# Group norm by ScalarE inside a recurrence, and a gate applied to turned tiles

## The chip, the cores and the metric

One core of a Trainium2 chip runs the whole program: a stack of transformer layers over 512 tokens of width 1,024. The metric is the device time of one execution in microseconds; the kernel before is given by the median of three runs, and its profile is one further execution.

## The reference, cut to what matters

The change lies in the first mixer, RWKV-7, of 16 heads with 64 features each. After the recurrence has made `y`, each head of each token is normed, scaled, given a bonus and a gate, and projected:

```
_, y = lax.scan(_rwkv7_step, S0, ...)              # S = S*w + (S a) b^T + v k^T ; y = S r
ym = y.mean(-1); yv = square(y - ym).mean(-1)      # over the 64 features of a head
yn = (y - ym) * rsqrt(yv + GN_EPS) * lnx_g + lnx_b
bonus = sum(r * k * r_k, -1) * v
g = sigmoid(xg @ g1) @ g2
x = layernorm(ALPHA * x + (1 + gt1) * ((yn + bonus) * g) @ w_out)
```

`gt1` and the shift and scale of the next layer come from a modulation vector `silu(c) @ ada_w + ada_b`, of which four parts of 1,024 columns are summed during the recurrence.

## The kernel before, in words

Three blocks follow one another for this mixer, with a barrier of all engines between them. `rwkv_project` makes receptance, key, value, decay and gate. `rwkv_chunks` runs the recurrence in four turns `t` of 128 tokens. `rwkv_finish` does what comes behind it. Then the feed-forward layer `ffn0` starts. Each engine has its own instruction stream, written out by hand, with semaphores between them; nothing is reordered.

In a turn of `rwkv_chunks` TensorE transposes three operands, forms products with 64x64 matmuls, inverts a triangular matrix in five levels (`LEVELS`), and then forms `UT`, the new state and the output. VectorE masks and adds between these products. ScalarE only copies: three transposed operands (L1365), the output of the turn before (`take_output`, L1370, into `Y`), two halves of `LT` (L1380), `ZA` (L1382, during the first level) and, after the last level, four pieces of `UT` (L1386), which TensorE needs for its next products. Between the `ZA` copy and the `UT` copies it has no work. `take_output(3)` stands behind the last turn and ends the block.

In `rwkv_finish` TensorE first sums the modulation over partitions (eight products with `ones`, L1531). VectorE takes the four tiles `t` of 128 tokens one after the other through a norm of twelve instructions (L1595 to L1614), six in `moments` and six behind them, with ScalarE's square root between. GpSimd multiplies `V` by the bonus factors `BON` (L1521). For each gated tile TensorE does eight transposes (L1541), ScalarE copies them out (L1570, `oT`), and TensorE does 16 products of 512 columns with `w_out` (L1549). `deepnorm_rows` (L531 to L541) then norms the rows on VectorE, beginning after all four tiles are gated. Every operand of L1549 is plain float32, and the profile has two matmul rows for each such product.

## Time and profile before

| | us |
|---|---|
| median of three runs | 2758.96 |
| lowest and highest of them | 2757.99, 2761.84 |
| the profiled execution's own time | 2755.7 |
| its span, first to last instruction | 2753.9 |
| the recurrence, `rwkv_chunks` | about 264 to 504.5 |
| `rwkv_finish` | about 504.7 to 593 |

The page of the profile gives the busy share of the span as 92% for TensorE, 75% for VectorE, 36% for ScalarE and 14% for GpSimd. Those are means over stages with different limits. Times below are counted from the span's start. A row of the timeline has the start, the time and what was idle before with its releaser; consecutive alike instructions stand in one row with their number, so a row of 32 matmuls is 16 products.

### The profile page before, as it was taken

The page shows a single profiled execution, that of the slowest core. Times are in us where ns is not written, and L with a number is a line of the kernel's source. Part 1 is how long each engine was busy: PE and PEld are TensorE (multiplying, and loading weights), DVE is VectorE, ACT ScalarE, POOL GpSimd, SP SyncE. Part 2 cuts the span into 40 slices and gives each one's busy share as a digit, 9 for nine tenths or more (in the row PEclk, how much of TensorE's full clock was granted, in tenths as well). Part 3 has the DMA queues.
Part 4 walks back from the last instruction along what each step waited for, and adds up shares of the span by engine and source line. Part 5 has one row for each costly group of instructions (what it writes and reads, how often), then busy time and mean ns, then how long its engine had stood idle before and what let it go on. Part 6 is the DMA issues. An engine that isn't in the chain of part 4 may idle for free. (4 is left out here: it accounts for less than half of the span.)

```text
span 2753.9 us, 42542 instructions
## 1 busy us (share of the span) xinstructions
PE 2546.2 (92%) x17194; PEld 2000.7 (73%) x17194; DVE 2055.5 (75%) x2896; ACT 989.2 (36%) x1075; POOL 390.5 (14%) x211
## 2 busy tenths in 40 slices
PE   5999988889999989999999988998998999999993
PEld 3785888558888854467788877886578788888883
DVE  6873666788777638778777766985846899999994
ACT  2632111122220023442222004333222777777772
POOL 1000000100000020000000000000002366656651
PEclk8999999999999999999999998999998999999997
DMA  5221122327663281204665323321407899999973
GB/s 209 81 82 41 65 80 80 139 79 227 183 187 126 84 257 53 77 31 136 215 184 174 116 79 112 92 77 47 153 1 260 316 369 372 371 368 360 367 299 129
DMA packets 247801, 459.91 MB, mean 167 GB/s; under 512 B 31125, under 2 KB 205869, under 8 KB 232297
## 3 DMA queue, kind: packets, MB, share of 16 engines
q1 hardware_dynamic: 227592, 433.41, 45.2%
q0 software_dynamic: 14384, 24.25, 2.6%
q8 instruction: 108, 1.77, 0.3%
q10 hardware_dynamic: 5682, 0.20, 0.1%
q14 instruction: 35, 0.29, 0.0%
HBM read 457.28 MB, written 30.56 MB: 177 GB/s over the span
## 5 line engine op out<-in xcount | busy, mean ns | idle before, releaser
L49 PE MATMUL ffn_bank<-ffn_xT_high,ffn_wi_high 128*128 128x512 f32 x704 | 275.4, 391 | 4.2 <-DVE stay_z_r L43 2.7
L50 PE MATMUL ffn_bank<-ffn_xT_low,ffn_wi_high 128*128 128x512 f32 x704 | 275.2, 391 | 0.0
L3304 POOL DMA_INDIRECT expert_rows<-exp_ys,exp_to_row x32 | 155.5, 4861 | 45.3 <-issue 44.4
L49 PEld LDWEIGHTS ffn_bank<-ffn_xT_high,ffn_wi_high 128*128 128x128 f32 x704 | 132.5, 188 | 32.2 <-DVE stay_z_r L43 3.3
L50 PEld LDWEIGHTS ffn_bank<-ffn_xT_low,ffn_wi_high 128*128 128x128 f32 x704 | 132.3, 188 | 28.3
L43 DVE TENSOR_TENSOR moe_u_low<-moe_u,exp_u_high 128x4096 fp32r<-128x4096 f32 x32 | 141.6, 4426 | 13.2 <-ACT exp_u_high L3378 12.8
L43 DVE TENSOR_TENSOR moe_g_low<-moe_g,moe_g_high 128x4096 fp32r<-128x4096 f32 x32 | 141.6, 4425 | 8.8 <-ACT moe_g_high L3378 8.6
L43 DVE TENSOR_TENSOR moe_d_low<-moe_d,exp_d_high 128x4096 fp32r<-128x4096 f32 x32 | 141.4, 4419 | 0.0
L51 PE MATMUL ffn_bank<-ffn_xT_high,stay_z_r 128*128 128x512 f32 x352 | 139.8, 397 | 0.0
L51 PE MATMUL ffn_bank<-ffn_wo_high,ffn_act_low 128*128 128x512 f32 x352 | 138.0, 392 | 0.0
L49 PE MATMUL ffn_bank<-ffn_wo_high,ffn_act_high 128*128 128x512 f32 x352 | 137.7, 391 | 0.0
L51 PE MATMUL ffn_bank<-ffn_xT_high,ffn_wi_low 128*128 128x512 f32 x352 | 137.2, 390 | 0.0
L3378 ACT CAST moe_g_high<-moe_g 128x4096 fp32r<-128x4096 f32 x31 | 112.8, 3639 | 64.4 <-PE exp_p_g L51 64.4
L3378 ACT CAST exp_u_high<-moe_u 128x4096 fp32r<-128x4096 f32 x32 | 116.4, 3637 | 3.8 <-PEq L2997 3.8
L3378 ACT CAST exp_d_high<-moe_d 128x4096 fp32r<-128x4096 f32 x32 | 116.6, 3643 | 1.1 <-DMA moe_d<-in_w_e_down 1.1
L3288 POOL COPY exp_from_row<-exp_rows 128x2 int32 (+1 forms) x30 | 107.9, 3596 | 10.5 <-PE exp_p_x L3332 6.5
L49 PE MATMUL exp_p_g<-moe_g_high,moe_xT_high 128*128 128x512 f32 x256 | 103.3, 404 | 3.2 <-DVE moe_xT_low L43 2.4
L49 PE MATMUL exp_p_y<-exp_d_high,exp_aT_high 128*128 128x512 f32 x256 | 104.5, 408 | 1.9 <-issue 1.9
L49 PE MATMUL hyb_bank<-stay_h_high,hyb_wb_high 128*128 128x512 f32 x256 | 104.1, 407 | 2.2 <-DVE stay_z_r L43 2.2
L363 ACT CAST ffn_wi_high<-ffn_wi 128x2048 fp32r<-128x2048 f32 x22 | 42.0, 1909 | 175.0 <-DMA ffn_wi<-in_ffn_w_in 175.0
L50 PE MATMUL hyb_bank<-hyb_hT_low,hyb_wb_high 128*128 128x512 f32 x256 | 102.7, 401 | 0.0
L49 PE MATMUL exp_p_u<-exp_u_high,moe_xT_high 128*128 128x512 f32 x256 | 100.3, 392 | 2.3 <-DVE moe_u_low L43 2.3
(710 smaller groups left out, 6615.0 us busy)
## 6 DMA issues: line engine op xcount, KB each, us to landing
moe_g<-in_w_e_gate SPq DMA_DIRECT2D x32, 2048.0 KB, 9.7
moe_u<-in_w_e_up SPq DMA_DIRECT2D x32, 2048.0 KB, 9.7
moe_d<-in_w_e_down SPq DMA_DIRECT2D x32, 2048.0 KB, 9.5
ffn_nw<-in_ada_w SPq DMA_DIRECT2D x24, 1024.0 KB
ffn_nw<-in_w_ada SPq DMA_DIRECT2D x24, 1024.0 KB
stay_z<-in_ffn_w_in SPq DMA_DIRECT2D x44, 512.0 KB, 5.1
ffn_wi<-in_ffn_w_in SPq DMA_DIRECT2D x44, 512.0 KB, 5.2
chunks_ada<-in_ada_w SPq DMA_DIRECT2D x16, 1024.0 KB, 5.1
```

What stands on the lines that cost most here:

```text
L43: return engine.tensor_tensor(low, x, high.bitcast(F32), ALU.subtract)
L49: nc.tensor.matmul(out, w[0], x[0], start=start, stop=False, **kw)
L50: nc.tensor.matmul(out, w[0], x[1], start=False, stop=False, **kw)
L51: return nc.tensor.matmul(out, w[1], x[0], start=False, stop=stop, **kw)
L363: nc.scalar.copy(wi_high[h][:, :, :, :], wi[h][:, :, :, :]).then_inc(s["wi_highs"], 1)
L3288: nc.gpsimd.tensor_copy(from_row[h][:, :, :], rows[:, bass.ds(n, 1), :]).then_inc(s["from_copied"], 1)
L3304: nc.gpsimd.indirect_dma_start(ys_dram, bass.IndirectOffsetOnAxis(ap=to_row[h][:, 0, 1:2].bitcast(U32), axis=0), ys[h][:, :], None, bounds ...
L3378: nc.scalar.copy(flat(high_of(name, h)[:, :, :]), flat(raw[name][h][:, :, :])).then_inc(s[f"{name}_high"], 1)
```

## The change

The gate `G` is formed transposed (features on partitions, tokens along the row): the two factors of its products change places. Inside the recurrence ScalarE now multiplies `V` by the bonus factors into `KT`, 16 heads a turn (`bonus`), takes mean and squares of the output of the turn before with accumulating activations and one square root (`moments`), and norms the output of two turns before (`normed`); VectorE makes two small rows for it (`scales`). This serves tiles 0 to 2; the norm of tile 3 stays in `rwkv_finish` on VectorE, with ScalarE's square. There TensorE turns both the normed tile and the bonus tile (16 transposes a tile instead of 8), ScalarE applies `lnx_g` and `lnx_b` as scale and bias of activations while it copies out (`affine`), VectorE adds the turned bonus and multiplies by `G` (`gate`), and the result is the operand of the same 16 products. `lnx_g` and `lnx_b` come as 8 rows of 128 each and are turned once; `w_out` comes in four pieces. The products themselves are plain float32 as before. The gates of tiles 2 and 3 stand between the row norms (`ahead`).

```diff
...
-                    nc.tensor.matmul(out[:, :], hid[:, 0, t * P:(t + 1) * P], g2a[:, half * HALF:(half + 1) * HALF], start=True, stop=False)
-                    last = nc.tensor.matmul(out[:, :], hid[0:R_G2, 1, t * P:(t + 1) * P], g2b[:, half * HALF:(half + 1) * HALF],
...
+                    nc.tensor.matmul(out[:, :], g2a[:, q * P:(q + 1) * P], hid[:, 0, :], start=True, stop=False)
+                    last = nc.tensor.matmul(out[:, :], g2b[:, q * P:(q + 1) * P], hid[0:R_G2, 1, :], start=False, stop=True)
...
-                nc.scalar.copy(G[:, q % 4, (q // 4) * HALF:(q // 4 + 1) * HALF], arrived("G", q)[:, :]).then_inc(act_took, 1)
+                nc.scalar.copy(G_xs[:, q, :], arrived("G", q)[:, :]).then_inc(act_took, 1)
...
+            def bonus(t):
+                act.wait_ge(s["k_psum"], 2 * t + 2)
+                for h in range(HEADS):
+                    q, e = divmod(h, 2)
+                    last = nc.scalar.activation(KT[:, q, t * P + e * HD:t * P + (e + 1) * HD], V[:, t, h * HD:(h + 1) * HD], ACT.Copy,
+                                                scale=BON[:, t, h:h + 1])
+                last.then_inc(s["bonus_done"], 1)
+            def moments(t):
+                act.wait_ge(s["y_done"], 2 * t + 2)
+                for h in range(HEADS):
+                    if h >= SPARES:
+                        act.wait_ge(s["mean_done"], HEADS * t + h - SPARES + 1)
+                    nc.scalar.activation(spare[:, h % SPARES, :], Y[:, t, h * HD:(h + 1) * HD], ACT.Copy, scale=-1.0 / HD,
+                                         accum_out=nmean[:, t, h:h + 1]).then_inc(s["mean_done"], 1)
+                act.wait_ge(s["mean_done"], HEADS * (t + 1))
+                for h in range(HEADS):
+                    if h >= SPARES:
+                        act.wait_ge(s["square_done"], HEADS * t + h - SPARES + 1)
+                    nc.scalar.activation(spare[:, h % SPARES, :], Y[:, t, h * HD:(h + 1) * HD], ACT.Square, bias=nmean[:, t, h:h + 1],
+                                         accum_out=rstd[:, t, h:h + 1]).then_inc(s["square_done"], 1)
+                act.wait_ge(s["square_done"], HEADS * (t + 1))
+                act.wait_ge(s["eps_set"], 1)
+                nc.scalar.activation(rstd[:, t, :], rstd[:, t, :], ACT.Sqrt, scale=1.0 / HD, bias=gn_eps[:, :]).then_inc(s["root_done"], 1)
+            def normed(t):
+                act.wait_ge(s["scaled_done"], 2 * t + 2)
+                for h in range(HEADS):
+                    part = Y[:, t, h * HD:(h + 1) * HD]
+                    last = nc.scalar.activation(part, part, ACT.Identity, scale=rstd[:, t, h:h + 1], bias=nmean[:, t, h:h + 1])
+                last.then_inc(s["norm_done"], 1)
...
+                bonus(t)
                 act.wait_ge(s["z_psum"], t + 1)
                 nc.scalar.copy(ZA[:, :, :, 0, :], pC[:, :, :].rearrange("p e (q i) -> p e q i", i=HD)).then_inc(s["z_done"], 1)
+                if t:
+                    moments(t - 1)
+                if t > 1:
+                    normed(t - 2)
...
+            normed(NT - 2)
             take_output(NT - 1)
...
+            def scales(t):
+                dve.wait_ge(s["root_done"], t + 1)
+                nc.vector.reciprocal(rstd[:, t, :], rstd[:, t, :]).then_inc(s["scaled_done"], 1)
+                dve.wait_ge(s["scaled_done"], 2 * t + 1)
+                nc.vector.tensor_tensor(nmean[:, t, :], nmean[:, t, :], rstd[:, t, :], ALU.mult).then_inc(s["scaled_done"], 1)
+            nc.vector.memset(gn_eps[:, :], GN_EPS).then_inc(s["eps_set"], 1)
...
+                if t > 1:
+                    scales(t - 2)
                 if t:
                     next_state(2 * t - 2)
...
+            scales(NT - 2)
             next_state(NC - 2)
...
-            sp.dma_start(lnx_g[:, :], spread(w["lnx_g"])).then_inc(lnx_loaded, 16)
...
-            sp.dma_start(w_out, w["w_out"].rearrange("(q p) n -> p q n", p=P)).then_inc(w_loaded, 16)
+            for n, name in enumerate(("lnx_g", "lnx_b")):
+                sp.dma_start(lnx_rows[n * KD:(n + 1) * KD, :], w[name].rearrange("(q p) -> q p", p=P)).then_inc(lnx_loaded, 16)
+            for i in range(4):
+                sp.dma_start(w_out[:, 2 * i:2 * i + 2, :], w["w_out"].rearrange("(q p) n -> p q n", p=P)[:, 2 * i:2 * i + 2, :]).then_inc(w_loaded[i], 16)
+            sp.dma_start(x_first, x_in.rearrange("(t p) d -> p t d", p=P)).then_inc(loaded, 16)
             sp.dma_start(g[:, :], spread(ln_g)).then_inc(v_loaded, 16)
             sp.dma_start(b[:, :], spread(ln_b)).then_inc(v_loaded, 16)
...
+            def turned(t):
+                if t:
+                    pe.wait_ge(z_done, KD * t)
+                    pe.wait_ge(z_added, 2 * t)
+                if t == LAST:
+                    pe.wait_ge(last_normed, 1)
+                for n in range(KD):
+                    nc.tensor.transpose(bank[4 + n // 4][:, (n % 4) * P:(n % 4 + 1) * P], Y[:, t, n * P:(n + 1) * P], ident[:, :])
+                for n in range(KD):
+                    last = nc.tensor.transpose(bank[6 + n // 4][:, (n % 4) * P:(n % 4 + 1) * P], bonus[:, n, t * P:(t + 1) * P], ident[:, :])
+                last.then_inc(turn_psum, 1)
+            pe.wait_ge(lnx_loaded, 32)
+            nc.tensor.transpose(bank[0][:, 0:2 * KD], lnx_rows[:, :], ident[0:2 * KD, 0:2 * KD]).then_inc(lnx_psum, 1)
+            turned(0)
             pe.wait_ge(ones_set, 1)
             for n in range(8):
                 lanes = P if n < 2 else 1
...
+                if n == 3:
+                    pe.wait_ge(lnx_done, 1)
+                elif n > 3:
+                    pe.wait_ge(mod_took, n - 3)
+                nc.tensor.matmul(bank[(n + 1) % 4][0:lanes, :], ones[:, 0:lanes], acc[:, n * HALF:(n + 1) * HALF], start=True, stop=True).then_inc(mod_psum, 1)
             for t in range(NT):
+                if t + 1 < NT:
+                    turned(t + 1)
                 pe.wait_ge(gated, t + 1)
                 if t == 0:
...
-                        last = nc.tensor.transpose(bank[6 + j][:, n * P:(n + 1) * P], Y[:, t, (4 * j + n) * P:(4 * j + n + 1) * P], ident[:, :])
...
+                    pe.wait_ge(mod_took, 8)
+                elif t > 1:
+                    pe.wait_ge(var_done, t - 1)
+                toks = slice(t * P, (t + 1) * P)
                 for j in range(NH2):
+                    cols = slice(j * HALF, (j + 1) * HALF)
                     for n in range(KD):
...
+                        if t == j == 0:
+                            pe.wait_ge(w_loaded[n // 2], 16)
+                        last = nc.tensor.matmul(bank[2 * (t % 2) + j][:, :], bonus[:, n, toks], w_out[:, n, cols], start=(n == 0), stop=(n == KD - 1))
                     last.then_inc(y_psum, 1)
...
+            def affine(t):
+                act.wait_ge(turn_psum, t + 1)
+                if t > 1:
+                    act.wait_ge(gated, t - 1)
+                for n in range(KD):
+                    nc.scalar.activation(z[:, t % 2, n, :], bank[4 + n // 4][:, (n % 4) * P:(n % 4 + 1) * P], ACT.Identity,
+                                         scale=lnx[:, n:n + 1], bias=lnx[:, KD + n:KD + n + 1]).then_inc(z_done, 1)
...
+            act.wait_ge(centred, 1)
+            nc.scalar.activation(z[:, 1, :, :].rearrange("p k n -> p (k n)"), Y[:, LAST, :], ACT.Square).then_inc(squared, 1)
+            act.wait_ge(lnx_psum, 1)
+            nc.scalar.copy(lnx[:, :], bank[0][:, 0:2 * KD]).then_inc(lnx_done, 1)
+            act.wait_ge(lnx_done, 1)
+            affine(0)
+            act.wait_ge(gn_var, 1)
+            nc.scalar.activation(rvar, rvar, ACT.Sqrt).then_inc(gn_root, 1)
+            for n in range(8):
+                take_mod(n)
+            act.wait_ge(mod_took, 8)
+            act.dma_start(mod.rearrange("(a n) -> a n", a=1)[:, 3 * D:6 * D], row[:, :]).then_inc(row_stored, 16)
+            affine(1)
             row_root(0)
...
+            affine(2)
+            row_root(1)
+            affine(3)
+            row_root(2)
+            row_root(3)
...
+            last = Y[:, LAST, :]
+            link(nc.vector.tensor_reduce(mean, H(last), AX.X, ALU.add))
+            link(nc.vector.tensor_scalar(mean, mean, 1.0 / HD, None, ALU.mult))
+            nc.vector.tensor_tensor(H(last), H(last), wide(mean), ALU.subtract).then_inc(centred, 1)
+            dve.wait_ge(squared, 1)
+            link(nc.vector.tensor_reduce(rvar, H(z[:, 1, :, :].rearrange("p k n -> p (k n)")), AX.X, ALU.add))
+            nc.vector.tensor_scalar(rvar, rvar, 1.0 / HD, GN_EPS, ALU.mult, ALU.add).then_inc(gn_var, 1)
+            def gate(t):
+                dve.wait_ge(turn_psum, t + 1)
+                for j in range(2):
+                    part = z[:, t % 2, 4 * j:4 * j + 4, :]
+                    dve.wait_ge(z_done, KD * t + 4 * j + 4)
+                    nc.vector.tensor_tensor(part, part, bank[6 + j][:, :].rearrange("p (n t) -> p n t", n=4), ALU.add).then_inc(z_added, 1)
+                dve.wait_ge(z_added, 2 * t + 2)
+                both = z[:, t % 2, :, :]
+                nc.vector.tensor_tensor(bonus[:, :, t * P:(t + 1) * P], both, G[:, :, t * P:(t + 1) * P], ALU.mult).then_inc(gated, 1)
+            gate(0)
+            dve.wait_ge(gn_root, 1)
+            link(nc.vector.reciprocal(rvar, rvar))
+            nc.vector.tensor_tensor(H(last), H(last), wide(rvar), ALU.mult).then_inc(last_normed, 1)
+            gate(1)
...
+            def ahead(t):
+                if t in (1, 2):
+                    gate(t + 1)
+                elif t == LAST:
+                    dve.wait_ge(affine_loaded, 32)
+                    link(nc.vector.tensor_scalar(sc[:, :], sc[:, :], 1.0, None, ALU.add))
+            deepnorm_rows(nc, dve, link, lambda t, j: bank[2 * (t % 2) + j], y_psum, x_first, gt, Y, g, b, (v_loaded, 16 * 2), st, mv, rstd, var_done, root, normed, x, ahead)
...
```

ScalarE in the third turn of the recurrence (`t` = 2), before: `chunks_LT` to `chunks_UT` are its copies of this turn.

```order
L1370 COPY rwkv_Y<-chunks_pC 128x8x64 x2
L1380 COPY chunks_LT<-chunks_pA 128x2x256
L1380 COPY chunks_LT<-chunks_pD 128x2x256
L1382 COPY chunks_ZA<-chunks_pC 128x16x64
L1386 COPY chunks_UT<-chunks_pA 128x512 x2
L1386 COPY chunks_UT<-chunks_pB 128x512 x2
```

The same place after; `rwkv_KT` now holds the bonus.

```order
L1409 COPY rwkv_Y<-chunks_pC 128x8x64 x2
L1419 COPY chunks_LT<-chunks_pA 128x2x256
L1419 COPY chunks_LT<-chunks_pD 128x2x256
L1376 ACTIVATE rwkv_KT<-rwkv_V,rwkv_BON 128x64 x16
L1422 COPY chunks_ZA<-chunks_pC 128x16x64
L1386 ACTIVATE chunks_spare,rwkv_nmean<-rwkv_Y 128x64 x16
L1392 ACTIVATE chunks_spare,rwkv_rstd<-rwkv_Y,rwkv_nmean 128x64 x16
L1396 ACTIVATE rwkv_rstd<-rwkv_rstd,chunks_gn_eps 128x16
L1403 ACTIVATE rwkv_Y<-rwkv_Y,rwkv_nmean,rwkv_rstd 128x64 x16
L1430 COPY chunks_UT<-chunks_pA 128x512 x2
L1430 COPY chunks_UT<-chunks_pB 128x512 x2
```

Sixteen activations have come ahead of the `ZA` copy, and 49 between it and the `UT` copies. Sixteen more of L1403 stand behind the last `UT` copies of the fourth turn, ahead of the last L1409.

TensorE at the start of `rwkv_finish`, before: the modulation (L1531), then transposes (L1541) and products (L1549) of tiles 0 and 1.

```order
L1531 MATMUL mixed_bank<-stay_acc,mixed_ones 128x512 x2
L1531 MATMUL mixed_bank<-stay_acc,mixed_ones 1x512 x6
L1541 MATMUL mixed_bank<-stay_ident,rwkv_Y 128x128 x8
L1549 MATMUL mixed_bank<-rwkv_AR,rwkv_KT 128x512 x16
L1541 MATMUL mixed_bank<-stay_ident,rwkv_Y 128x128 x8
L1549 MATMUL mixed_bank<-rwkv_AR,rwkv_KT 128x512 x16
```

The same place after: the names are those of the turned vectors, the normed tile, the bonus tile, the modulation and the products.

```order
L1601 MATMUL mixed_bank<-stay_ident,mixed_lnx_rows 128x16
L1595 MATMUL mixed_bank<-stay_ident,rwkv_Y 128x128 x8
L1597 MATMUL mixed_bank<-stay_ident,rwkv_KT 128x128 x8
L1610 MATMUL mixed_bank<-stay_acc,mixed_ones 128x512 x2
L1610 MATMUL mixed_bank<-stay_acc,mixed_ones 1x512 x6
L1595 MATMUL mixed_bank<-stay_ident,rwkv_Y 128x128 x8
L1597 MATMUL mixed_bank<-stay_ident,rwkv_KT 128x128 x8
L1625 MATMUL mixed_bank<-rwkv_AR,rwkv_KT 128x512 x16
L1595 MATMUL mixed_bank<-stay_ident,rwkv_Y 128x128 x8
L1597 MATMUL mixed_bank<-stay_ident,rwkv_KT 128x128 x8
L1625 MATMUL mixed_bank<-rwkv_AR,rwkv_KT 128x512 x16
```

The transposes of tile 0 have moved ahead of the modulation, and those of each later tile ahead of the products of the tile before it.

## Rows read from the trace of the kernel before

**Rows 1.** Windows, last turn and finish: PE, PEld, DVE, ACT, POOL busy; PEclk, DMA, GB/s.

```profile
443.00:504.50 61.50, 55.46 (x1771) 53.43 (x1769) 37.90 (x50) 8.50 (x13) 0.00 (x0) 0.97 0.06 21
504.50:593.10 88.60, 70.10 (x176) 30.91 (x176) 79.29 (x93) 11.88 (x25) 10.76 (x7) 0.91 0.30 107
```

**Rows 2.** Timeline of TensorE in the finish: start, us, engine, line, what.

```profile
504.98 7.22 PE L1531 MATMUL mixed_bank<-stay_acc,mixed_ones 128*128 128x512 f32 x16 [1.64 <-POOL mixed_ones L1519]
...
521.60 1.97 PE L1541 MATMUL mixed_bank<-stay_ident,rwkv_Y 128*128 128x128 f32 x8 [9.39 <-DVE rwkv_Y L1614]
...
524.24 5.98 PE L1549 MATMUL mixed_bank<-rwkv_AR,rwkv_KT 128*128 128x512 f32 x8 [0.67 <-ACT rwkv_KT L1570]
...
555.96 1.04 PE L1541 MATMUL mixed_bank<-stay_ident,rwkv_Y 128*128 128x128 f32 x8
...
557.73 14.00 PE L1549 MATMUL mixed_bank<-rwkv_AR,rwkv_KT 128*128 128x512 f32 x32 [0.73 <-ACT rwkv_KT L1570]
...
573.33 14.00 PE L1549 MATMUL mixed_bank<-rwkv_AR,rwkv_KT 128*128 128x512 f32 x32 [0.73 <-ACT rwkv_KT L1570]
```

**Rows 3.** Timeline, recurrence end and first tile: the other engines.

```profile
498.27 0.68 DVE L1456 TENSOR_TENSOR rwkv_AR<-rwkv_AR,chunks_pB 128x512 f32<-128x512 f32 x1
...
503.38 1.07 ACT L1370 COPY rwkv_Y<-chunks_pC 128x512 f32<-128x512 f32 x2 [10.40 <-PE chunks_pC L1210]
...
504.76 1.22 DVE L1595 TENSOR_REDUCE mixed_mean<-rwkv_Y 128x16 f32<-128x1024 f32 x1 [2.71 <-PEq L1190]
...
515.00 0.25 DVE L1608 RECIPROCAL mixed_var<-mixed_var 128x16 f32<-128x16 f32 x1 [0.54 <-ACT mixed_var L1565]
...
520.32 1.22 DVE L1614 TENSOR_TENSOR rwkv_Y<-rwkv_Y,rwkv_G 128x1024 f32<-128x1024 f32 x1
```

**Rows 4.** Timeline of ScalarE in the third turn of the recurrence.

```profile
401.97 1.01 ACT L1382 COPY chunks_ZA<-chunks_pC 128x1024 f32<-128x1024 f32 x1 [8.89 <-PE chunks_pC L1210]
426.49 1.07 ACT L1386 COPY chunks_UT<-chunks_pA 128x512 f32<-128x512 f32 x2 [23.51 <-PE chunks_pA L1210]
428.24 1.07 ACT L1386 COPY chunks_UT<-chunks_pB 128x512 f32<-128x512 f32 x2 [0.67 <-PE chunks_pB L1210]
```

**Rows 5.** Timeline of TensorE in that turn: first product that reads `UT`.

```profile
430.69 0.32 PE L1210 MATMUL chunks_pB<-stay_z,chunks_UT 64*64 64x128 f32 x1
```

**Rows 6.** Groups of ScalarE by shape: number, busy us, mean ns of one.

```profile
L1999 ACT ACTIVATE dsa_ckv<-dsa_bank 128x128 f32<-128x128 f32 x4 | 1.1, 277 | 7.3 <-PE dsa_bank L1829 7.3
...
L1999 ACT ACTIVATE dsa_qT<-dsa_bank 128x512 f32<-128x512 f32 x8 | 4.8, 597 | 50.2 <-PE dsa_bank L1829 50.2
...
L1991 ACT ACTIVATE dsa_hT<-dsa_bank,stay_sh,stay_sc 128x512 f32<-128x512 f32 x8 | 6.0, 776 | 6.8 <-PE dsa_bank L1804 6.5
...
L2045 ACT ACTIVATE dsa_L<-dsa_L,dsa_nmax 128x128 f32<-128x128 f32 x16 | 6.2, 387 | 0.0
...
L2045 ACT ACTIVATION_READ_ACCUMULATOR dsa_L<-dsa_L,dsa_nmax 128x1 f32 x64 | 12.0, 188 | 0.0
```

**Rows 7.** Timeline of ScalarE where accumulating activations follow one another.

```profile
1126.16 0.39 ACT L2045 ACTIVATE dsa_L<-dsa_L,dsa_nmax 128x128 f32<-128x128 f32 x1
...
1126.56 0.61 ACT L2045 ACTIVATE dsa_L<-dsa_L,dsa_nmax 128x384 f32<-128x384 f32 x1
```

**Rows 8.** Windows around two idle stretches of TensorE; columns as in rows 1.

```profile
515.00:521.60 6.60, 0.00 (x0) 0.00 (x1) 6.43 (x7) 0.00 (x0) 1.11 (x2) 0.52 1.02 412
...
528.00:529.00 1.00, 1.00 (x3) 0.44 (x2) 0.96 (x2) 0.00 (x0) 0.00 (x0) 0.56 1.17 313
...
595.00:597.00 2.00, 1.96 (x10) 1.99 (x11) 1.57 (x8) 1.99 (x3) 1.06 (x2) 0.50 0.14 38
...
600.00:601.00 1.00, 1.00 (x8) 1.00 (x7) 0.97 (x3) 0.92 (x2) 0.00 (x0) 0.72 1.10 374
```

**Rows 9.** Issues of small transfers at the program's start: KB, us to landing.

```profile
stay_ident<-in_ident SPq DMA_DIRECT2D x1, 64.0 KB, 2.3
...
rwkv_cond<-in_c SPq DMA_DIRECT2D x1, 4.0 KB, 1.6
```

More of the change, by code:

```diff
@@ L525, in deepnorm_rows @@
     for t in range(NT):
+        if ahead is not None:
+            ahead(t)
         for j in range(NH2):
@@ L1456, in _ @@
                     nc.vector.tensor_tensor(AR[:, :, 1, toks], AR[:, :, 1, toks], both[:, :, 0, :], ALU.add).then_inc(s["rg_done"], 1)
+            scales(NT - 2)
             next_state(NC - 2)
 def rwkv_finish(nc, room, buf, Y, acc, stay, next_w_in, z_loaded, x_in, mod, w, ln_g, ln_b):
[L1462 to L1463 removed]
+    LAST = NT - 1
+    flat = lambda v: v[:, :, :, :].rearrange("p q a t -> p q (a t)")
+    w_out = flat(buf["AR"])
+    bonus = buf["KT"]
+    G = buf["G"][:, :, :].rearrange("p t (a n) -> p (t a) n", n=T)
+    mean, rvar = (buf[n][:, LAST, :] for n in ("nmean", "rstd"))
     x, ident, sc, sh = (stay[n] for n in ("x", "ident", "sc", "sh"))
     x_first = buf["BT"][:, :, :].rearrange("p (t a) n -> p t (a n)", t=NT)
[L1466 to L1467 removed]
+    z = room.sb("z", [P, 2, KD, P])
     gt = room.sb("gt", [P, D])
@@ L1481, in rwkv_finish @@
     loaded = room.sem("loaded")
-    w_loaded = room.sem("w_loaded")
+    w_loaded = [room.sem(f"w_loaded{i}") for i in range(4)]
     v_loaded = room.sem("v_loaded")
```

106 lines of the change are left out of this document (23 added, 83 removed).

## The prediction

> **What bounds the kernel now.** I read the windows by stage first. The finish lasts from 504.5 to 593.1, and in it VectorE is busy for 79.3 of 88.6 us and TensorE for 70.1; in the last turn of the recurrence TensorE has 55.5 of 61.5 and ScalarE 8.5 [rows 1]. So the two stages have different limits, and only the finish has VectorE as a candidate. Then I read the finish in order of time. TensorE does the modulation until 512.2, waits 9.39 us for the first gated tile, which VectorE ends at 521.5, and from 521.60 it never waits for VectorE again: the tiles follow each other every 15.60 us (557.73 to 573.33), and the last product ends at 573.33 + 14.00 = 587.33 [rows 2, 3]. VectorE's norm is therefore on the path only up to 521.6. Behind that TensorE is the bound, and VectorE's later norms lie beside it. The reader is to see that most of the VectorE work that the change takes away from the finish costs nothing today.
>
> Third, ScalarE in the recurrence: before the `ZA` copy it idles 8.89 us, between that copy and the first `UT` copy 23.51 us [rows 4]. The `UT` copies end at 429.31 and TensorE reads them at 430.69, a slack of 1.4 us [rows 4, 5].
>
> **The transposed gate.** As many products and copies of the same sizes in the projection: nothing, from both sides, since only which factor is the weight changes. The output products were plain float32 before and still are; that part of the title moves nothing.
>
> **ScalarE in the recurrence.** The trace has no 64-column activation, so I build one. Without operands by partition 128 columns take 277 ns and 512 take 597, hence 0.833 ns a column and 224 ns for 64. A scale and a bias by partition add 776 - 597 = 179 ns: 403. One such operand, from the 387 ns at 128 columns: 334. Reading an accumulator takes 188 [rows 6]. Activation and read start again after 0.40 us although their durations sum to 0.575, so each overlaps its neighbour by 87 ns [rows 7]. Start to start this gives 247 ns for a bonus, 224 + 188 - 174 = 238 for a mean, 348 for a square and 316 for a norm. A turn then has 16 bonuses = 4.0 us in the 8.89; and 3.8 + 5.6 for the moments, 0.3 for the root and 5.1 for the norm of the tile before = 14.8 us in the 23.51. Without any overlap it is 16 x (412 + 522 + 403) + 0.3 = 21.7 us, still inside. I take the overlapped price, since rows 7 are the nearest. The cost in the turns is nothing, and the cover is the five levels on TensorE and VectorE; if it were gone, each us over 23.5 + 1.4 would delay the `UT` copies, and TensorE with them. VectorE's small rows at the start of a turn lie where it waits for TensorE's state product.
>
> The trace says that ScalarE has the room. The Trainium skill, "ScalarE: Activation LUTs", section "Rules for kernel authors", speaks against the move: additions and multiplications belong on VectorE, not ScalarE. In the same page, "What ACT_TABLE_LOAD costs" gives 186 ns plus 0.833 ns a column, about 93 ns for each pointer operand, and 93 ns of overlap; by that the norm is 332 ns start to start, an estimate, against my 316 from rows, and the tail below would be 0.3 us longer.
>
> **The tail of the recurrence.** The norm of tile 2 stands after the last turn and ahead of the last output copy. It waits for VectorE's last addition, which ends at 498.95, and two small rows of 0.25 [rows 3]: ScalarE starts at 499.5, needs 16 x 0.316 = 5.1 and then 1.07 for the copy, to 505.7. Before, the copy ended at 504.45. Queued behind the waiting norm is that copy alone, and behind it the barrier. Cost 1.2 us; from both sides 0 (0.2 us each would hide it) and 2.5 (no overlap, 403 ns). The finish then starts at S = 505.7 + 0.3 = 506.0, where the 0.3 is the distance of 504.45 and 504.76 before.
>
> **The start of the finish.** The first wait is now the load of the two turned vectors: small transfers on this queue land 1.6 to 2.3 us after issue [rows 9], so S + 2.3 with the second issued a little later. TensorE has then been idle since the state's last product, ended before 503.38, some 5 us. What idleness does is in the rows: after the modulation's end at 512.2 the mean granted clock from 515.0 to 521.6 is 0.52, so it had fallen to the lower level (1.2 GHz) soon after 515, 3 us into the idleness. It was 0.56 from 528 to 529, so it rose near 528.9, 7.3 us after the restart at 521.6; in the next layer it was 0.50 at the restart at 595.0 and 0.72 from 600 to 601, so it rose 5.4 after [rows 8]. I take 6.3, S + 8.6. The 17 transposes at 1.97 / 8 [rows 2] last 4.2, to S + 6.5. VectorE's centring and ScalarE's square are ready before (three passes over a tile of 1.22 or less [rows 3]). ScalarE's eight affine activations (277 + 179 - 87 = 369 ns each) end at S + 9.6, the root and the first modulation copy at S + 10.5. The modulation is 0.9 us a product at the full clock [rows 2] and 1.8 at half: products 0 to 3 end at S + 11.2, after the first copy freed a bank, and 4 to 7 at S + 14.8, with ScalarE's 0.6 us copies keeping pace. The transposes of tile 1, twice 1.04 with an overlap, 1.9, end at S + 16.6. VectorE's first gate is done by S + 13. `w_out` needs 4 MB at the 412 GB/s of [rows 8], about 10 us, and is first of the large transfers now; it lands near S + 13.5. So the first product starts at S + 16.6 = 522.6, against 524.24 [rows 2]: 1.6 us earlier.
>
> **The body of the finish.** A tile's products take 15.60 - (557.73 - 555.96) = 13.83 us [rows 2]. Of the 1.77 between, 0.73 was the wait for ScalarE's copy and the rest the eight transposes. Now 16 transposes stand there, 1.9, without the wait: even. What does go is the last gap, since nothing is turned ahead of tile 3, and the low clock of the first products, 524.24 to 528.9, which the modulation now absorbs. So 3 x 13.83 + 14.0 + 2 x 1.9 = 59.3, and the last product ends at 522.6 + 59.3 = 581.9, against 587.33. VectorE's gates (two passes of half a tile, one of a whole) and row norms fit into 15.7 us a tile; the row norm behind the last product is as before.
>
> **The sum.** 587.33 - 581.9 = 5.4 us, rounded 5.5: the profiled execution's 2755.7 becomes 2750.2. That execution lies 3.3 us under the median of the runs, 2758.96, so on that scale the forecast is 2753.5. Its own range, from the norm without overlap (-4) to a clock that rises at once (-7.5), is 2751.5 to 2755.
>
> **The rivals.**
> The clock is kinder: TensorE does not lose it over the 5 us of idleness. The 17 transposes then take 2.0, the first copy frees its bank at S + 8.3, the modulation ends at S + 11.9 and the first product starts at S + 13.8: 2.8 us more, 8.2 in all, 2750.8, and with the tail's norm hidden 9.4, 2749.6. For it speaks only that two restarts differ by 2 us in when they rise; against it, that both stretches in rows 8 fell 3 us into idleness.
>
> ScalarE is dearer per instruction, since moments wait on their own semaphores and no row shows that: at 0.5 us each the turns still hide it (49 x 0.5 = 24.5), but the tail is 4.1 us late and the gain 2.6: 2756.4.
>
> ScalarE becomes what the recurrence waits for, which ends on the other side. Its place is the 49 activations ahead of the `UT` copies in turns 2 and 3. From 0.50 us each they pass 23.5 + 1.4; at 0.6 each turn is 4.8 us late, the tail 16 x 0.6 - 3.9 = 5.7, together 15.3 against 6.7 that the finish gives without the tail: 8.6 slower, 2767.6. It decides from 0.53 us, and by 0.57 exceeds a measurable loss. Against it: even without overlap the mean is 0.446. This is how the skill's rule above would be right.
>
> The modulation keeps TensorE at half clock, waiting for ScalarE's copies between products: eight at 1.8 end at S + 20.9, tile 1's transposes at S + 25.1, and the first products lose 2.6 as before. The last product ends at 593: 5.7 slower, 2764.7; half of it is no change. Against it, TensorE runs without a gap from S + 2.3 to S + 11, longer than either rise took.
>
> **How the numbers follow.** Forecast 0.50; kinder clock 0.18; dearer ScalarE 0.14; clock lost in the modulation 0.08; ScalarE the bound 0.10. About 0.2% (5.5 us) is what a measurement of this kernel can tell from no change, and the forecast lies on that line, so I halve it: faster 0.25 + 0.18 = 0.43; same 0.25 + 0.14 + 0.04 = 0.43; slower 0.04 + 0.10 = 0.14. The range goes from 2748.5, just beyond the kinder clock, to 2760.5, which takes in the dearer ScalarE and the lower half of the lost clock.
>
> **What would show it.** In the profile after: the small activations at about 0.25 to 0.35 us start to start, and `UT` copies that still begin when TensorE's products end; the last output copy ending near 505.7; the first product of the finish near 522.6 and the clock back at 1.00 before it; tiles 15.7 us apart; the last product near 582. The forecast is wrong if ScalarE is the releaser of TensorE in turns 2 or 3, if TensorE waits for a gate after the first tile, or if the granted clock is still low in the first products.

## The result and the profile after

The changed kernel takes 2742.53 us (median of seven runs, 2738.8 to 2749.91) against 2758.96, a ratio of 0.994 with the 95% interval 0.9924 to 0.9956. Over this and the later sets of runs it is 2743.2 on average (18 runs), and the kernel before 2757.7 in the later ones (101 runs): 14.5 us faster. I had forecast 5.5. One run of before_rec, at 3266.3 us and a mean granted clock of 0.741, was slow and is left out of its median and average below.

| profiled execution | before | after |
|---|---|---|
| own time / span, us | 2755.7 / 2753.9 | 2738.8 / 2737.0 |
| mean granted TensorE clock | 0.968 | 0.971 |
| busy us: TensorE, VectorE, ScalarE, GpSimd | 2546, 2056, 989, 391 | 2541, 2022, 1056, 382 |
| recurrence's last product to next layer's first transpose | 91.7 | 83.3 |
| from there to the next layer's first weight product | 6.1 | 5.0 |
| from there to the end of the span | 2152.7 | 2143.0 |

The last line is the surprise: 9.7 us are gained in code that is the same in both kernels.

The changed blocks first. Windows of the last turn and of the finish, columns as in [rows 1]:

```profile
445.50:507.95 62.45, 54.95 (x1769) 53.24 (x1768) 38.24 (x52) 32.59 (x126) 0.00 (x0) 0.97 0.06 20
507.95:587.20 79.25, 71.25 (x209) 34.36 (x209) 44.54 (x64) 17.48 (x47) 1.30 (x3) 0.97 0.30 107
```

ScalarE's work in the turn rises from 8.5 to 32.6 us, and the turn is hardly longer: from its first transpose to the recurrence's last product it takes 63.8 us, before 63.4. VectorE's in the finish falls from 79.3 to 44.5, and the finish is 9.4 us shorter. The timeline of TensorE in the finish, against [rows 2]:

```profile
509.90 0.23 PE L1601 MATMUL mixed_bank<-stay_ident,mixed_lnx_rows 16*128 16x16 f32 x1 [4.16 <-DMA mixed_lnx_rows<-in_rwkv_lnx_b]
510.06 1.88 PE L1595 MATMUL mixed_bank<-stay_ident,rwkv_Y 128*128 128x128 f32 x8
511.73 1.91 PE L1597 MATMUL mixed_bank<-stay_ident,rwkv_KT 128*128 128x128 f32 x8
513.44 7.45 PE L1610 MATMUL mixed_bank<-stay_acc,mixed_ones 128*128 128x512 f32 x16
...
522.62 13.90 PE L1625 MATMUL mixed_bank<-rwkv_AR,rwkv_KT 128*128 128x512 f32 x32
...
538.11 13.90 PE L1625 MATMUL mixed_bank<-rwkv_AR,rwkv_KT 128*128 128x512 f32 x32
...
553.59 27.63 PE L1625 MATMUL mixed_bank<-rwkv_AR,rwkv_KT 128*128 128x512 f32 x64
589.02 5.20 PE L272 MATMUL ffn_bank<-stay_ident,stay_x 128*128 128x128 f32 x32 [7.80 <-PEq L97]
```

The first product starts at 522.62, the tiles follow every 15.49 us, and the last product ends at 581.22. That looks like my 522.6, 15.7 and 581.9, but in this execution the recurrence ended 2.4 us later than in the trace of before (505.73 against 503.34; the end differs from one execution of a kernel to the next, and a second trace of before has 505.73 too). Counted from that end, the first product comes after 16.9 us (forecast 19.3, before 20.9). ScalarE, against [rows 3, 4]; first the waits for TensorE ahead of the `UT` copies, then the tail:

```profile
428.52 1.07 ACT L1430 COPY chunks_UT<-chunks_pA 128x512 f32<-128x512 f32 x2 [8.60 <-PE chunks_pA L1214]
...
501.33 5.41 ACT L1403 ACTIVATE rwkv_Y<-rwkv_Y,rwkv_nmean,rwkv_rstd 128x64 f32<-128x64 f32 x16 [6.38 <-DVE rwkv_nmean L1464]
506.65 1.05 ACT L1409 COPY rwkv_Y<-chunks_pC 128x512 f32<-128x512 f32 x2
```

The 23.51 us of idleness became 8.60, and TensorE still ends it.

### The profile page after: what moved, and what is told of

The parts are those of the page before. It is cut to its first block and busy times, and to the rows that moved or that the text cites. A ratio compares the mean times of both kernels' runs of the same rounds, so it can differ in the third digit from the quotient of the medians.

```text
span 2737.0 us, 42916 instructions
## 1 busy us (share of the span) xinstructions
PE 2541.4 (93%) x17227; PEld 1996.7 (73%) x17227; DVE 2022.1 (74%) x2874; ACT 1055.9 (39%) x1405; POOL 382.1 (14%) x207
## 3 DMA queue, kind: packets, MB, share of 16 engines
q8 instruction: 108, 1.77, 0.3%
## 5 line engine op out<-in xcount | busy, mean ns | idle before, releaser
L3392 POOL DMA_INDIRECT expert_rows<-exp_ys,exp_to_row x32 | 153.7, 4805 | 45.3 <-issue 44.5
```

The costliest lines, as they stand in the source:

```text
L3392: nc.gpsimd.indirect_dma_start(ys_dram, bass.IndirectOffsetOnAxis(ap=to_row[h][:, 0, 1:2].bitcast(U32), axis=0), ys[h][:, :], None, bounds ...
```

## The experiments

**Is it luck? Both kernels again, and both delayed.** In the traces at hand, short stretches at half the clock lie at different places behind the finish. One pair of windows shows such a stretch (columns as above), of before:

```profile
1695.00:1699.60 4.60, 2.46 (x11) 1.67 (x9) 4.53 (x4) 3.42 (x4) 0.00 (x0) 1.00 0.13 20
1699.60:1703.00 3.40, 3.31 (x8) 2.63 (x9) 2.33 (x2) 2.20 (x3) 0.00 (x0) 0.51 0.89 286
```

and the same work in the changed kernel:

```profile
1687.00:1691.60 4.60, 2.46 (x11) 1.66 (x9) 4.53 (x4) 3.43 (x4) 0.00 (x0) 1.00 0.12 26
1691.60:1695.00 3.40, 3.31 (x14) 2.74 (x15) 2.32 (x2) 2.19 (x3) 0.00 (x0) 1.00 0.86 273
```

The stall of 2.23 us ahead is the same, yet only in the first does the clock drop to its lower level, and 8 products are done instead of 14. So four runs: each kernel unchanged, and each with this at the end of the finish's vector work:

```diff
+            for _ in range(6):
+                link(nc.vector.memset(gt[:, :], 0.0))
```

> The kernel before, once more, for a second trace of it and for the granted clock beside each of its times. In the traces at hand the next layer starts 6.0 us earlier after the change, but the span is 16.9 us shorter; about 11 us come up behind the changed blocks, in code that is the same. Much of it sits at short stretches in which the granted clock is 0.5: before has them near 1700, 1877, 1914, 1942, 2132 and 2142 us, after near 1885, 1917 and 1949. Theory P (position): whether a stall of some 2 us is followed by such a stretch depends on the moment at which the stall comes, and the moment is the same in every execution; then this trace shows the stretches at the same six places within 1 us, and the time is 2756 to 2761. Theory N (luck between executions): they lie elsewhere in each execution; then this trace has them at other places, single times scatter by some 10 us with the mean clock, and at equal clock this kernel stands 6 us above the changed one. Theory C (carried over: the changed blocks leave something behind that makes later stages faster, such as another placement of tiles or of instructions): the same places as before, 2756 to 2761.

> The changed kernel, once more. Theory P: the stretches at half clock again near 1885, 1917 and 1949 us and none after the 2.2 us stall at 1689 to 1691; 2739 to 2746. Theory N: at other places, times from 2738 to 2752 in step with the mean granted clock (0.967 to 0.973), and 6 us under the kernel before at equal clock. Theory C: the same places as after, 2739 to 2746.

> The changed kernel with six fills of a 128x1024 tile at the end of the finish's vector work, behind its last row norm. A fill of 128x512 took 0.485 us in the trace of before, so six of twice the size are some 5.7 us (an estimate), and the next layer starts where it starts in the kernel before, near 594.7 us. Theory P: all later stages then stand at the moments of the kernel before, and most of the extra gain is gone: 2754 to 2759. Theory C: only the delay is added, 2742.5 + 5.7 = 2748.2, with the stretches at half clock at the same stalls as in the changed kernel. Theory N: 2748 on average, with single times from 2744 to 2757.

> The kernel before with the same six fills at the end of its finish. Theories C and N: 2759 + 5.7 = 2764.7 (N: single times 2761 to 2772). Theory P: the stalls come at new moments, so the time is off that sum by several us in either direction: 2755 to 2761 or 2768 to 2772.

Measured: before_again 2758.84 (ratio to before 1.0003, 0.9994 to 1.0011), after_again 2742.8 (0.9947, 0.9934 to 0.996). The second trace of before has no low clock at 1699, but others at 265 and 381 us that the first lacks. So the places change between executions of one program: theory N is right about single traces, and the 11 us between my first two traces were partly luck. The difference of the medians is not luck, since it came again in each of three sets of runs. The fills delay the next layer by 6.7 us in before and about 7.5 in after; the averages rise by 5 (median 2763.14) and by 11 (2754.33, single runs from 2743 to 2759). Before pays no more than was added, as C and N have it. After pays 3 us more than that, and its median lies in the range of theory P; the mean granted clock of its runs is lower too, 0.9671 against 0.9696 without the fills. Why, and why the runs spread so widely, stays open.

**The place of the instruction packets.** The traces showed one thing that did not change between executions. In the hybrid stage (the layer behind the second feed-forward layer, tiles `hyb`) a 1 MB weight load is waited for, and it lands in 6.5 to 6.8 us in the three traces of before (before, before_again, before_late6) and in 5.5 to 5.6 in the three of after. Before: the wait for it and its landing, and the DMA queues in one microsecond of it, with packets, MB and share.

```profile
  ACT hyb_wb_high L2515: 5.9, 1
...
DMA to landing us min/median/max: 6.5/6.5/6.5
```

```profile
q1 hardware_dynamic: 368, 0.38, 106.2%
q8 instruction: 1, 0.02, 6.5%
```

In the changed kernel the load is alone, with the packet some 8 us ahead of it; the wait is 5.0 us instead of 5.9. Its landing, and the queues meanwhile:

```profile
DMA to landing us min/median/max: 5.6/5.6/5.6
...
DMA packets 1040, 1.05 MB, mean 218 GB/s; under 512 B 16, under 2 KB 1040, under 8 KB 1040
## 3 DMA queue, kind: packets, MB, share of 16 engines
q1 hardware_dynamic: 1040, 1.05, 70.7%
```

Before, one packet of instructions shares the DMA engines with the load (108 packets carry 1.77 MB on this queue, 16 KB each). Where TensorE runs steady products of 0.23 us, the packets come 30 us apart, the time of some 128 products with their weight loads, so I take them for TensorE's. The change adds 33 transposes, 33 weight loads and takes two waits away; every packet behind it comes earlier. The test adds instructions that do nothing where TensorE idles anyway:

```diff
                     last.then_inc(y_psum, 1)
+            for _ in range(128):
+                pe.wait_ge(ones_set, 1)
```

(two such waits make one instruction: the trace has 65 more of TensorE's; after_fetch192 has 192 waits here and 96 behind each of the two feed-forward stages).

> The kernel before with 64 more instructions in TensorE's stream that do no work: waits on a semaphore that has long been reached, behind the last product of the finish, where TensorE idles 7.7 us anyway. The change adds 33 transposes with as many weight loads and takes two waits away, 64 instructions. What is disputed: behind the finish the hybrid stage takes 407.6, 406.2 and 408.1 us in the three traces of the kernel before and its delayed form, and 402.0, 402.5 and 403.9 in those of the changed one, in the same code. In all three of before one packet of the instruction queue falls into the middle of a 1 MB weight load that is waited for, which lands in 6.5 to 6.8 us; in all three of the changed one the packet comes before the load, which lands in 5.5 to 5.6. Theory F (fetch): the places of these packets follow the count of instructions ahead, and moving them alone gives most of the 4 us: the packet leaves the load, it lands in 5.5 to 5.7, the hybrid stage takes 402 to 404.5, and the time is 3 to 4.5 under before: 2753 to 2755.5. Theory P (only the moment in time counts, for the clock): nothing moves, 2757.5 plus or minus 1.5, hybrid stage 406 to 408. Theory W (another wait or the placement of tiles of the changed blocks does it): also 2757.5, and the load still lands in 6.5 or more or lands sooner without gain.

> The changed kernel with some 192 more idle instructions in TensorE's stream (96 behind the finish, 48 behind each of the two feed-forward stages, where TensorE waits 8 us or more for the next stage), so that the packets of the instruction queue stand about where they stand in the kernel before: 64 + 192 = 256, and in stretches of steady products one packet comes every 30 us, or 128 products with their weight loads. Theory F: the packet is back in the weight load of the hybrid stage, which lands in 6.5 or more; the hybrid stage takes 405 to 408 and the time is 3 to 4.5 over the changed kernel, 2746 to 2747.5. Theories P and W: 2743 plus or minus 1.5. If the packet comes to lie elsewhere (the count is an estimate from the pitch), the run says nothing against F as long as the load then lands in 5.5.

Measured: before_fetch64 2752.03 (0.9978, 0.9968 to 0.9988), after_fetch192 2747.39 (0.9968, 0.9956 to 0.998, where after has 0.9947): on average, idle instructions make the old kernel 5.1 us faster and the new one 4.6 slower. The packet moved as expected. In before_fetch64 the loads of that stretch land so:

```profile
DMA to landing us min/median/max: 5.5/5.5/6.0
```

after_fetch192:

```profile
DMA to landing us min/median/max: 5.7/6.7/6.7
```

Theories P and W fall. Over 18 traces the hybrid stage takes 407.0 us (405.8 to 408.1) in the seven with the packet in the load, and 404.0 (400.5 to 407.9) in the other eleven. ScalarE waits 9.9 to 11.6 us for the loads of that stretch in the seven, and 7.3 to 9.3 in the eleven. So 3 of the 5 us lie there. The two traces that don't fit, after_third (407.9) and after_best_again (407.8), both with no load over 5.8, have the longest time at the lower clock in that stage: 33.7 and 32.4 us, against 16.0 to 30.4 in the other sixteen.

The other 2 us go with the clock of the whole run. Within either kernel a run is longer the lower its mean granted clock (before: 2760.4 us on average at 0.964, 2755.0 at 0.968), by a fit over both kernels some 1.5 us for each 0.001. The idle instructions raise the mean clock from 0.9658 to 0.9675 in before, and in after they lower it from 0.9696 to 0.9686: 2.6 and 1.5 us by that slope, an estimate. Why the clock follows the place of the instructions is not shown.

The Trainium skill, "Runtime: NRT & Kernel Launch", section "Instruction fetch mechanics", says that instructions are fetched in 16 KiB blocks of 256 and that the cost of crossing a block is "mostly hidden". The blocks and their spacing agree with these traces; the cost was not hidden from a load that was waited for, 6.5 us against 5.6.

**The finish: tail, clock and ScalarE.** after_tail forms the small rows for tile 2 ahead of VectorE's last modulation pass; after_warm puts idle transposes ahead of TensorE's first wait; after_best has the change of after_tail and ten idle transposes behind the recurrence's last product; after_double takes all moments twice. The cuts below are, in order, of after_tail (two), after_warm, after_best and after_double (which does the same with the squares).

```diff
                 else:
+                    scales(NT - 2)
                     add_modulation(15, 1)
...
-            scales(NT - 2)
             next_state(NC - 2)
...
+            keep_busy(nc, bank[1], ident, 14)
             pe.wait_ge(lnx_loaded, 32)
...
+            keep_busy(nc, pA[:, 0, :], stay["ident"], 10)
...
+                for r in range(2):
+                    for h in range(HEADS):
```

> The changed kernel with the small rows for tile 2 on VectorE ahead of its last modulation pass instead of behind the last turn; ScalarE's norm of tile 2 then starts right behind the UT copies (it idled 6.4 us there) instead of at 501.33, and no longer holds up the last output copy. By my step on the tail the norm cost 1.2 us, of which the trace shows 0.9 (norm done 506.7, TensorE's last product 505.7): 1 us faster, 2741.5 to 2742. Rival: the finish starts earlier but the load of the two turned vectors and the clock decide, and nothing is gained: 2742.5 to 2743.

> The changed kernel with 14 idle transposes (some 1.9 us at the full clock) ahead of TensorE's first wait in the finish. In the changed kernel TensorE restarts at 509.9, the granted clock is 0.5 from about 511 to 513.5, and the 17 transposes take 3.7 us. My prediction had put the low clock at 6.3 us from the restart. If the fall comes from the idle stretch of 3 to 4 us ahead, it is gone with the filler, the transposes take 2 us, and the gain is up to 1.7 us: 2741 to 2742. Rival: the weight loads or ScalarE's affine work decide the first product, and nothing is gained: 2742.5 to 2743.5.

> The changed kernel with every mean and every sum of squares on ScalarE taken twice (32 more activations with accumulator in each of the turns 1 to 3, the same values again): at 0.24 and 0.33 us start to start, 9.1 us more in a turn. ScalarE idles 12.6 us ahead of the first UT copy in turn 1 and 8.6 in turns 2 and 3, waiting for TensorE. My step says the turns hide it: at most 0.5 us a turn comes out, 2743 to 2744.5. The rival that ScalarE becomes the bound would show 9 us in each of two or three turns: 2761 to 2770.

> The changed kernel with the earlier small rows of after_tail and ten idle transposes on TensorE right behind the last product of the recurrence, while ScalarE still copies the last output, so that TensorE is idle for 2 us less ahead of the finish. If the granted clock then stays at its higher level, the 17 transposes take 2 us instead of 3.7 and the finish is 1.5 to 2.5 us shorter: 2740.5 to 2741.5. Rival: the clock falls all the same, or the affine work on ScalarE sets the first product: 2742.5 to 2744.

after_tail: 2743.66 (0.9946, 0.9931 to 0.9961), nothing gained in time, although from the recurrence's last product to the next layer it takes 82.1 us instead of 83.4. after_warm: 2746.25 (0.9957, 0.9944 to 0.997): the clock had fallen at 507, one us ahead of the filler, which then ran for 3.2 us at half the clock and held up the transposes; a miss: this filler began 3 us into the idleness, and too late. after_double: 2741.87 (0.9946, 0.9933 to 0.9959); 9 us more on ScalarE in each of three turns cost nothing that its six runs show (2742.7 on average). Its rows in the third turn show the cover used up, no wait being left ahead of the `UT` copy:

```profile
423.24 5.40 ACT L1405 ACTIVATE rwkv_Y<-rwkv_Y,rwkv_nmean,rwkv_rstd 128x64 f32<-128x64 f32 x16
428.54 1.05 ACT L1432 COPY chunks_UT<-chunks_pA 128x512 f32<-128x512 f32 x2
```

**What gives the finish its 8 us.** before_rec is the old finish with the norm of tiles 0 to 2 on ScalarE in the recurrence; before_rec_fetch has the idle instructions too; before_nopool takes only the bonus off GpSimd; before_rec_nopool both. The first cut below is of the two without GpSimd's bonus, the others are of the three with the norm in the recurrence.

```diff
-            for t in range(NT):
-                nc.gpsimd.tensor_tensor(H(V[:, t, :]), H(V[:, t, :]), wide(BON[:, t, :]), ALU.mult).then_inc(bonus_done, 1)
...
+            moments(NT - 1)
...
-                moments(t)
...
+                if t == NT - 1:
```

> The recurrence part of the change alone: ScalarE forms moments and norm of tiles 0 to 2 inside the recurrence, as in the changed kernel; the bonus stays on GpSimd, the finish stays in its old form (gate not transposed, output turned after gating) and VectorE only normalizes tile 3 in it, first of all. TensorE has exactly as many instructions as in the kernel before, so the instruction packets stay where before has them and this run measures the work itself. By rows: the finish starts about 1 us later (norm of tile 2 in the tail); VectorE needs 5.2 us for the moments of tile 3 and 4 passes of 1.22 for tile 0, which is gated about 10.5 us into the finish instead of 16.7; transposes and copy 2.7; w_out behind 1 MB of norm vectors lands some 14.5 us in. First product about 16.8 us behind the recurrence's last product instead of 20.9: 4 us faster, 2753 to 2754.5. The weight load of the hybrid stage lands in 6.5 or more as in before. Rival: the 9.4 us for which TensorE waits in before come off in full, 2749; or the norm on ScalarE delays the turns, over 2758.

> The same with the idle instructions of before_fetch64 behind the finish. If both effects are real and separate they add: 2753.5 - 5 = 2748.5 (plus or minus 1.5). If the fetch of instructions had been a matter of the moment in time, this run gives before_rec's time again.

> The kernel before with one part of the change: the bonus is formed by ScalarE inside the recurrence, and GpSimd's four multiplications at the start of the finish (9.44 us from 504.98) are gone. Everything else is as in before, TensorE's instruction count too. Theory G (GpSimd slows VectorE): in before VectorE's first passes take 2.88 and 2.81 us and its two small rows 0.90 and 0.50 while GpSimd multiplies, against 1.23, 1.23, 0.18 and 0.18 afterwards; without GpSimd the first tile is gated 3.3 + 1.0 = 4.3 us earlier, and TensorE's first output product comes 16.6 us behind the recurrence's last product instead of 20.9: 2753 plus or minus 1.5. Theory V (VectorE's passes are slow there for another reason, such as the loads landing at the same time): they stay at 2.8, and the time at 2757.5.

> The same together with moments and norm of tiles 0 to 2 on ScalarE, so that only the turned gate and the new order of the finish are missing from the change; before_rec took 2759 on average. Theory G: VectorE's moments of tile 3 take 5.4 us instead of 9.6, the first tile is gated 4.2 us earlier than in before_rec, and the first product comes some 15.5 us behind the recurrence's last one instead of 19.6: 2754 to 2755. If w_out, which stands behind 1 MB of norm vectors in the queue, lands later than that, it is 17 us and 2756.

before_rec: 2760.09 (1.0007, 0.9996 to 1.0018), a miss of some 6 us. Its timeline in the finish: GpSimd's multiplications, and VectorE's passes beside and after them.

```profile
507.98 9.44 POOL L1576 TENSOR_TENSOR rwkv_V<-rwkv_V,rwkv_BON 128x1024 f32<-128x1024 f32 x4
...
509.94 2.88 DVE L1649 TENSOR_TENSOR rwkv_Y<-rwkv_Y,mixed_mean 128x1024 f32<-128x1024 f32 x1
...
512.86 2.81 DVE L1650 TENSOR_TENSOR mixed_y<-rwkv_Y 128x1024 f32<-128x1024 f32 x1
515.70 1.22 DVE L1651 TENSOR_REDUCE mixed_var<-mixed_y 128x16 f32<-128x1024 f32 x1
```

The VectorE passes with two operands take 2.88 and 2.81 us as long as GpSimd multiplies, and 1.22 otherwise. before_nopool has 1.22 throughout, so theory G is right on the passes, and still nothing is gained: 2756.79 (0.9995, 0.9984 to 1.0006). The next waiter is in its row:

```profile
510.10 0.17 DVE L1609 TENSOR_SCALAR mixed_var<-mixed_var 128x16 f32<-128x16 f32 x1
516.79 0.25 DVE L1617 RECIPROCAL mixed_var<-mixed_var 128x16 f32<-128x16 f32 x1 [6.51 <-ACT mixed_var L1574]
```

The root of the variance stands on ScalarE behind eight copies of the modulation and a table load of 1.28 us. In this trace a stretch at half the clock makes the modulation 1.7 us longer than in before (8.90 against 7.22); without it the root would come about when before has it, so nothing would be gained even then (an estimate). before_rec_nopool is free of that wait as well, and shows a third waiter, `w_out` behind 1 MB of norm vectors in the queue:

```profile
519.14 1.32 PE L1595 MATMUL mixed_bank<-stay_ident,rwkv_Y 128*128 128x128 f32 x8 [4.55 <-DVE rwkv_Y L1666]
...
524.42 6.06 PE L1603 MATMUL mixed_bank<-rwkv_AR,rwkv_KT 128*128 128x512 f32 x7 [3.96 <-DMA rwkv_AR<-in_rwkv_w_out]
```

Its first product comes 19.7 us behind the recurrence, where 15.5 to 17 were expected. Its runs give 2753.72 (0.9979, 0.9971 to 0.9988), 5.4 us under the kernel before on average. That is near the forecast, but not by its path, so it is luck: only 0.7 of it is in the finish of its trace (91.0 against 91.7), and the packet lies in the load as in before. Some 3 us go with the mean clock of its runs, 0.9679 against 0.9658 (by the slope above); why it is higher stays open. before_rec_fetch: 2752.6 (0.998, 0.9971 to 0.9989), so the idle instructions are worth 6.1 us on average here too, though the 2748.5 expected fails with before_rec's forecast. The Trainium skill, "SBUF — State Buffer", section "Terms", says that VectorE and GpSimd share a pair of ports under an exclusive lock and that the loser "fully blocks"; the passes of 2.8 us agree that one holds up the other, while VectorE's reduction with one operand, at 515.70, kept its 1.22 beside GpSimd. That either stands still for a whole instruction of the other, no row here shows.

**The shortest start, again.**

> after_best once more. In its trace the stretch from the recurrence's last product to the next layer is 80.9 us, against 83.3 to 84.1 in the changed kernel, yet the runs gave 2743.0 on average as the changed kernel does. If the 2.5 us are real: 2740.5 plus or minus 1.5, under after_third of the same session. If the low clock merely moves to another place: the same as after_third.

> The changed kernel a third time, as the comparison for after_best_again: 2743 plus or minus 1.5, with 5.5 to 5.6 us for the hybrid stage's weight load.

after_best gave 2744.05 (0.9949, 0.9934 to 0.9964), then 2741.66 (0.9941, 0.9927 to 0.9956); after_third 2743.88 (0.9941, 0.9927 to 0.9955). In the second trace of after_best the transposes run at the full clock:

```profile
505.57 1.09 PE L1596 MATMUL mixed_bank<-stay_ident,rwkv_Y 128*128 128x128 f32 x8
506.50 1.04 PE L1598 MATMUL mixed_bank<-stay_ident,rwkv_KT 128*128 128x128 f32 x8
```

and from the recurrence's last product to the next layer it takes 80.8 us, 2.6 less than after's 83.4. (The 80.9 of the expectation counts from the end of the filler; from the recurrence's own last product the first trace has 82.2, and in it the clock fell at 510.6, as the second row of transposes began.) The average of the 12 runs of both is 2742.8, the changed kernel's 2743.2 (18 runs, standard error 0.9): a gain over the changed kernel is not shown.

## Why the prediction was wrong

The range ended at 2748.5 and the time is 2742.5. Two steps failed: the clock at the start of the finish came back sooner than I took it to, and the sum put the unchanged stages behind the finish at nothing. Point by point:

- *ScalarE in the recurrence: hidden.* Right. A mean comes every 0.24 us (forecast 0.238), a square every 0.33 (0.348), 16 norms take 5.41 (5.1); the estimate of 0.332 for a norm from the Trainium skill ("ScalarE: Activation LUTs", section "What ACT_TABLE_LOAD costs") is nearer to the measured 5.41 / 16 = 0.338 than mine of 0.316 from rows. The rival that ScalarE becomes the bound fell with after_double. (Its price was a little off too: 49 x 0.6 = 29.4 us is 4.5 over 24.9, not 4.8.)
- *The tail, 1.2 us.* Right: from TensorE's last product to the end of the last output copy it is now 2.0 us, before 1.1, a cost of 0.9.
- *The start of the finish: "I take 6.3, S + 8.6".* This step failed: in the windows of after the clock is back 3.6 us behind the restart at 509.9, and the modulation runs at the higher level. The reading of the restarts before (5.4 and 7.3 us) was right, but the clock fell only at 510.2 here, 4.5 us into the idleness and not 3.

```profile
510.50:513.50 3.00, 3.00 (x16) 3.00 (x15) 1.58 (x3) 1.12 (x2) 0.00 (x0) 0.50 0.95 348
513.50:515.00 1.50, 1.50 (x5) 0.60 (x4) 0.00 (x0) 1.25 (x4) 0.00 (x0) 0.96 0.91 366
```

  The transposes and the modulation thus take 10.9 us instead of 12.5, 1.6 less than forecast; the restart, 0.8 sooner, is the rest of the 2.4 us at the first product. Two traces of before have 13.7 us at the lower level from the wait for the first tile on; three of after have 3.4, 6.8 and 3.4 around the restart. From the recurrence's end to the next layer it is 91.7 us in three traces with the old finish and 83.3, 84.1 and 83.0 in after: 8.2 us, where the sum had 5.4. My rival of the kinder clock, at a chance of 0.18, gave 8.2 too. That the numbers meet is in part luck: its condition did not hold, since the clock did fall, for 3.4 us.
- *The body: even.* Right: 15.49 us a tile (forecast 15.7), and 58.6 from the first product to the end of the last (59.3).
- *The sum.* It went from the last product straight to the end, so everything behind counted as unchanged. This is the larger error. The 64 instructions that TensorE's stream gained move the instruction packets, and moving them is worth 4.6 to 6.1 us by the averages of three pairs of kernels, 5.1 in before_fetch64, which adds as many as the change. 8.2 + 5.1 = 13.3, against 14.5 measured, with a standard error of 0.9 on the changed kernel alone; more can't be told apart. The next layer's first transposes also gain 1.1 us (6.1 to 5.0), but nothing comes of it: that whole layer takes 386.2 and 386.0 us in two traces of before, and 386.8, 386.5 and 386.5 in after. I had counted each added transpose as time on TensorE and none as an instruction to be fetched. What stays open is how the packets do it beyond the load in the hybrid stage, and before_rec_nopool shows that a run can gain about as much outside its finish with TensorE's packets where they were.
- *Where the 8 us come from* I had right only in part. VectorE's norm was not what held up the first tile by itself: behind it stood GpSimd's hold on VectorE, ScalarE's order and the place of `w_out` in the queue. Taking the first of them, the norm or both away gained at most 0.7 us in the finish (91.2 in before_rec, 92.6 in before_nopool, 91.0 in before_rec_nopool, against 91.7). Of the 8.2 us, 4.0 are at the first product, 16.9 us behind the recurrence instead of 20.9; the body gives the rest, since its first products no longer run at half the clock and nothing is turned ahead of the last tile. No run moves `w_out` alone, so the share of each wait is not shown.

## What to carry to other kernels

Ask of a late stage's start not only which wait is last but how many waits stand behind it at nearly the same time: here three, and the runs that removed one or two of them gained next to nothing. A change that adds or removes instructions on a long stream can move every later fetch, so compare it with a version that has the same count of idle instructions before crediting the work, and compare the mean granted clock of the runs as well. And count a forecast's end at the end of the program, with a term for the unchanged stages, even if its value is zero with some width.

## What I had not expected of the hardware

- One 16 KB instruction packet in the middle of a 1 MB load goes with a landing of 6.5 to 6.8 us instead of 5.5, and moving the packet by idle instructions moves the landing (before_fetch64, after_fetch192).
- GpSimd's 128x1024 multiplications (2.36 us each on average) more than double VectorE's two-operand passes beside them, from 1.22 to 2.88 us.
- The same 2.23 us stall of TensorE is followed by 3.4 us at half the clock in one execution and not in another, and single runs of one program spread over 10 us, the longer the lower their mean clock (after: 2748.65 at 0.967, 2739.85 at 0.973).
